# Heads' last norm in an RWKV-7 layer: logarithms and exponentials in groups of four, gates and norm products moved to later steps

## The reference, cut to what matters

```python
mean = jnp.mean(ys, axis=-1, keepdims=True)
var = jnp.mean(jnp.square(ys - mean), axis=-1, keepdims=True)
yn = ((ys - mean) * lax.rsqrt(var + GN_EPS)).reshape(B, T, D)
yn = yn * p['rwkv_lnx_g'][i].astype(F32) + p['rwkv_lnx_b'][i].astype(F32)
bonus = (jnp.sum(rh * kh * p['rwkv_rk'][i].astype(F32), axis=-1, keepdims=True) * vh).reshape(B, T, D)
out = ((yn + bonus).astype(u.dtype) * g) @ p['rwkv_wo'][i]
```

## Time and profile before

| | |
|---|---|
| device time, median of 3 runs | 3728.64 us (3728.14 to 3729.97) |
| profiled execution: its time, its span | 3730.17 us, 3728.4 us |
| mean granted TensorE clock over the span | 0.949 |
| TensorE busy over the span | 3406.7 us, 91% |
| VectorE, ScalarE busy over the span | 1154.4 us (31%), 908.2 us (24%) |
| this stage: first mean product, end of the last product | 2651.83 us, 2877.88 us |
| its steps without a projection | 2651.8 to 2725.4 us |

### The profile page before, as it was taken

One profiled execution on the slowest core, in us unless ns is written; L12 is line 12 of the kernel. 1 busy time (PEld: TensorE's weight loads), 2 busy tenths in 40 slices (PEclk: granted clock), 3 DMA queues, 4 the chain that ended last, 5 costly groups with the idle time before them and its releaser, 6 DMA issues. The chain is left out here.

```text
span 3728.4 us, 65930 instructions
## 1 busy us (share of the span) xinstructions
PE 3406.7 (91%) x29166; PEld 2836.6 (76%) x29166; DVE 1154.4 (31%) x1968; ACT 908.2 (24%) x1542; POOL 460.2 (12%) x375
## 2 busy tenths in 40 slices
PE   5999687879999999979999699998899799999996
PEld 3667354559999999946555399998455799999995
DVE  1099653131111111151445333433232311112112
ACT  2001234122111111110245333332252311111111
POOL 0000110001122122100011111110000122122120
PEclk9999898889999999989999799999589899999998
DMA  2123342111111111112032322221300111111111
GB/s 79 51 49 96 123 159 92 34 34 40 46 49 48 37 54 46 35 35 87 31 135 104 124 45 55 51 46 50 122 0 1 46 41 51 42 52 49 37 46 61
DMA packets 171994, 222.35 MB, mean 60 GB/s; under 512 B 104739, under 2 KB 122916, under 8 KB 170692
## 3 DMA queue, kind: packets, MB, share of 16 engines
q1 hardware_dynamic: 159284, 174.42, 15.8%
q0 software_dynamic: 12432, 43.80, 3.3%
HBM read 180.63 MB, written 37.55 MB: 59 GB/s over the span
## 5 line engine op out<-in xcount | busy, mean ns | idle before, releaser
L2415 PE MATMUL f_out<-f_u_hi,f_weights_hi 128*128 128x352 f32 x2112 | 685.4, 325 | 48.0 <-DVE f_u_lo L2457 48.0
L2416 PE MATMUL f_out<-f_u_lo,f_weights_hi 128*128 128x352 f32 x2112 | 680.4, 322 | 0.0
L2417 PE MATMUL f_out<-f_u_hi,f_weights_lo 128*128 128x352 f32 x2112 | 679.9, 322 | 0.0
L2391 POOL TENSOR_TENSOR f_weights_lo<-f_weights,f_weights_hi 128x1024 fp32r<-128x1024 f32 (+2 forms) x168 | 323.1, 1924 | 1731.2 <-ACT f_weights_hi L2427 1731.2
L2415 PEld LDWEIGHTS f_out<-f_u_hi,f_weights_hi 128*128 128x128 f32 x2112 | 399.2, 189 | 50.2 <-issue 40.8
L1292 PE MATMUL rf_out<-rf_mixed,rf_weights 128*128 128x352 f32 (+2 forms) x1344 | 413.7, 467 | 24.0 <-DVE rf_mixed L1451 24.0
L2416 PEld LDWEIGHTS f_out<-f_u_lo,f_weights_hi 128*128 128x128 f32 x2112 | 399.7, 189 | 0.0
L2417 PEld LDWEIGHTS f_out<-f_u_hi,f_weights_lo 128*128 128x128 f32 x2112 | 398.7, 189 | 0.0
L1292 PEld LDWEIGHTS rf_out<-rf_mixed,rf_weights 128*128 128x128 f32 (+2 forms) x1344 | 246.9, 186 | 185.7 <-issue 49.6
L2415 PE MATMUL f_out<-f_inner_hi,f_weights_hi 128*128 128x352 f32 x1056 | 341.4, 323 | 4.0 <-DVE f_inner_lo L2488 4.0
L2480 DVE TENSOR_TENSOR f_product<-f_out,f_gate 128x352 f32<-128x352 f32 x132 | 69.3, 525 | 880.3 <-PE f_out L2417 880.3
(11 more groups left out here) (348 smaller groups left out, 4467.7 us busy)
## 6 DMA issues: line engine op xcount, KB each, us to landing
f_weights<-in_w_gu SPq DMA_DIRECT2D x88, 512.0 KB, 3.5
f_weights<-in_w_down SPq DMA_DIRECT2D x48, 256.0 KB, 2.6
rf_weights<-in_w_rkv SPq DMA_DIRECT2D x24, 512.0 KB, 3.6
f_weights<-in_w_down SPq DMA_DIRECT2D x32, 320.0 KB, 2.9
all_hT<-in_x SPq DMA_DIRECT2D x2, 4224.0 KB, 13.0
all_hT<-in_cache_k SPq DMA_DIRECT2D x32, 256.0 KB, 4.7
all_hT<-in_cache_k POOLq DMA_DIRECT2D x32, 256.0 KB, 4.3
all_hT<-in_cache_v SPq DMA_DIRECT2D x32, 256.0 KB, 3.6
```

The source lines that it names most:

```text
L2391: pool.tensor_tensor(lo[:, s, :w], raw[:, s, :w], hi[:, s, :w].bitcast(F32), ALU.subtract).then_inc(lo_ready, 1)
L2415: pe.matmul(out, hi[:, s, w], x_hi, start=(k == 0), stop=False)
L2416: pe.matmul(out, hi[:, s, w], x_lo, start=False, stop=False)
L2417: last = pe.matmul(out, lo[:, s, w], x_hi, start=False, stop=(k == parts - 1))
```

## The change

The step lags become GATE = 4, NORM = 5 and LAG = 14, with GROUP = 4. TensorE's step s is then mean_sum(s), gates(s-4), project(s-14), var_sum(s-1). VectorE's is centre(s+1), add(s-15), norm(s-5). ScalarE's is square(s+1), log(s), and in every fourth step the four exponentials of the group; before it was one logarithm and one exponential in each step. The ring of centred tiles has 10 slots in place of 4, the ring of roots 8 in place of 2. Each bonus tile has its own semaphore, and unit u < 8 waits for its tile alone. The number of instructions for data stays the same on every engine, and so do the DMAs and their order.

```diff
+GROUP = 4
...
     UNITS_ = NCH * KD
-    LAG = KD + 3
+    GATE, NORM, LAG = GROUP, GROUP + 1, KD + GROUP + 2
...
-        d, sq, stat = st.sb("centred", [P, 4, TC]), st.sb("sq", [P, 2, TC]), st.sb("stat", [P, 2, TC])
+        DB, SB = 2 * GROUP + 2, 2 * GROUP
+        d, sq, stat = st.sb("centred", [P, DB, TC]), st.sb("sq", [P, 2, TC]), st.sb("stat", [P, SB, TC])
...
+        bonus_in = [st.sem(f"bonus_loaded{i}") for i in range(KD)]
...
-                    sp.dma_start(bonus[:, i], scratch["bonus"][i]).then_inc(q_["bonus_loaded"], 16)
+                    sp.dma_start(bonus[:, i], scratch["bonus"][i]).then_inc(bonus_in[i], 16)
...
                     if s < UNITS_:
                         mean_sum(s)
-                    if 0 <= s - 1 < UNITS_:
-                        gates(s - 1)
+                    if 0 <= s - GATE < UNITS_:
+                        gates(s - GATE)
                     if s >= LAG:
                         project(s - LAG)
                     if 0 <= s - 1 < UNITS_:
...
+                def log(u):
+                    act.wait_ge(q_["var_sum"], u + 1)
+                    if u >= SB:
+                        act.wait_ge(q_["n1"], u - SB + 1)
+                    act.activation(stat[:, u % SB], var[u % 2][:, :TC], ACT.Ln, scale=1.0 / DH,
+                                   bias=K.gn_eps).then_inc(q_["log"], 1)
+
                 def root(u):
-                    act.wait_ge(q_["var_sum"], u + 1)
-                    if u >= 2:
-                        act.wait_ge(q_["n1"], u - 1)
-                    act.activation(stat[:, u % 2], var[u % 2][:, :TC], ACT.Ln, scale=1.0 / DH,
-                                   bias=K.gn_eps).then_inc(q_["log"], 1)
                     act.wait_ge(q_["log"], u + 1)
-                    act.activation(stat[:, u % 2], stat[:, u % 2], ACT.Exp, scale=-0.5).then_inc(q_["root"], 1)
+                    act.activation(stat[:, u % SB], stat[:, u % SB], ACT.Exp, scale=-0.5).then_inc(q_["root"], 1)
 
                 square(0)
-                for u in range(UNITS_):
-                    if u + 1 < UNITS_:
-                        square(u + 1)
-                    root(u)
+                for s in range(UNITS_):
+                    if s + 1 < UNITS_:
+                        square(s + 1)
+                    if s < UNITS_:
+                        log(s)
+                        if s % GROUP == GROUP - 1:
+                            for u in range(s - GROUP + 1, s + 1):
+                                root(u)
...
                     if u < KD:
-                        dve.wait_ge(q_["bonus_loaded"], 16 * KD)
+                        dve.wait_ge(bonus_in[u], 16)
...
                 for s in range(UNITS_ + LAG):
                     if s + 1 < UNITS_:
                         centre(s + 1)
-                    if s >= LAG:
-                        add(s - LAG)
-                    if s < UNITS_:
-                        norm(s)
+                    if s > LAG:
+                        add(s - LAG - 1)
+                    if 0 <= s - NORM < UNITS_:
+                        norm(s - NORM)
+                add(UNITS_ - 1)
```

More of the change, by code:

```diff
@@ L2142, in finish_heads @@
         g2, g2b = st.sb("gate2", [P, KD, P]), st.sb("gate2b", [G2, KD, P])
-        d, sq, stat = st.sb("centred", [P, 4, TC]), st.sb("sq", [P, 2, TC]), st.sb("stat", [P, 2, TC])
+        DB, SB = 2 * GROUP + 2, 2 * GROUP
+        d, sq, stat = st.sb("centred", [P, DB, TC]), st.sb("sq", [P, 2, TC]), st.sb("stat", [P, SB, TC])
         mean, var, gate, out = ([st.bank(f"{n}{s}") for s in range(2)] for n in ("mean", "var", "gate", "out"))
         q_ = {n: st.sem(n) for n in ("mean_sum", "centred", "sq", "var_sum", "log", "root", "n1", "n2", "gate", "gated",
-                                     "projected", "added", "gates_loaded", "bonus_loaded", "weights_loaded")}
+                                     "projected", "added", "gates_loaded", "weights_loaded")}
+        bonus_in = [st.sem(f"bonus_loaded{i}") for i in range(KD)]
         col = lambda n, i: vec[:, VEC.at[n]][:, i:i + 1]
@@ L2213, in square @@
                         act.wait_ge(q_["var_sum"], u - 1)
-                    act.activation(sq[:, u % 2], d[:, u % 4], ACT.Square).then_inc(q_["sq"], 1)
-                def root(u):
-                    act.wait_ge(q_["var_sum"], u + 1)
-                    if u >= 2:
-                        act.wait_ge(q_["n1"], u - 1)
-                    act.activation(stat[:, u % 2], var[u % 2][:, :TC], ACT.Ln, scale=1.0 / DH,
-                                   bias=K.gn_eps).then_inc(q_["log"], 1)
+                    act.activation(sq[:, u % 2], d[:, u % DB], ACT.Square).then_inc(q_["sq"], 1)
+                def log(u):
[4 more added lines that the diff above has]
+                                   bias=K.gn_eps).then_inc(q_["log"], 1)
+                def root(u):
                     act.wait_ge(q_["log"], u + 1)
-                    act.activation(stat[:, u % 2], stat[:, u % 2], ACT.Exp, scale=-0.5).then_inc(q_["root"], 1)
+                    act.activation(stat[:, u % SB], stat[:, u % SB], ACT.Exp, scale=-0.5).then_inc(q_["root"], 1)
                 square(0)
-                for u in range(UNITS_):
-                    if u + 1 < UNITS_:
-                        square(u + 1)
-                    root(u)
+                for s in range(UNITS_):
[6 more added lines that the diff above has]
+                                root(u)
             @block.vector
@@ L2235, in centre @@
                     dve.wait_ge(q_["mean_sum"], u + 1)
-                    dve.scalar_tensor_tensor(d[:, u % 4], mean[u % 2][:, :TC], -1.0 / DH, yT[:, i, cols],
+                    dve.scalar_tensor_tensor(d[:, u % DB], mean[u % 2][:, :TC], -1.0 / DH, yT[:, i, cols],
                                              ALU.mult, ALU.add).then_inc(q_["centred"], 1)
@@ L2241, in norm @@
                     dve.wait_ge(q_["root"], u + 1)
-                    dve.scalar_tensor_tensor(d[:, u % 4], d[:, u % 4], col("lnx_g", i), stat[:, u % 2],
+                    dve.scalar_tensor_tensor(d[:, u % DB], d[:, u % DB], col("lnx_g", i), stat[:, u % SB],
                                              ALU.mult, ALU.mult).then_inc(q_["n1"], 1)
                     if u < KD:
-                        dve.wait_ge(q_["bonus_loaded"], 16 * KD)
+                        dve.wait_ge(bonus_in[u], 16)
                     dve.wait_ge(q_["n1"], u + 1)
-                    dve.scalar_tensor_tensor(d[:, u % 4], d[:, u % 4], col("lnx_b", i), bonus[:, i, cols],
+                    dve.scalar_tensor_tensor(d[:, u % DB], d[:, u % DB], col("lnx_b", i), bonus[:, i, cols],
                                              ALU.add, ALU.add).then_inc(q_["n2"], 1)
@@ L2250, in norm @@
                     dve.wait_ge(q_["n2"], u + 1)
-                    dve.tensor_tensor(yT[:, i, cols], gate[u % 2][:, :TC], d[:, u % 4], ALU.mult).then_inc(q_["gated"], 1)
+                    dve.tensor_tensor(yT[:, i, cols], gate[u % 2][:, :TC], d[:, u % DB], ALU.mult).then_inc(q_["gated"], 1)
                 def add(w):
```

## The result

The changed kernel takes 3788.38 us (median of 4 runs, 3780.24 to 3789.89), the kernel before in the same session 3728.39 us. The ratio is 1.0161, 95% interval 1.0146 to 1.0177: 60 us slower. The forecast was 3783, range 3757 to 3799. All ratios here leave out one execution of the kernel with filler products (further on), which took 4505.87 us at a mean clock of 0.735, where its nine others took 3733 to 3744.

What follows compares the result with a forecast made beforehand. From 2725.4 on TensorE's own products bound the stage; before that, waits between engines. 2731.7 + 14.7 + 94.2 + 18.0 + 6.9 + 18.9 + 47.8 = 2932.2 against 2877.9, +54.3 us, hence 3783 us, range 3757 to 3799.

Steps and rivals of the forecast that it cites:

- The loop: Steps 6 to 23: TensorE's gate product waits for a norm queued behind centring that needs this step's mean; 8.09 us at half clock.
- The start and the first stretch: Steps 0 to 5 end at 2667; steps 6 to 13 at half clock take 64.7 us, so step 14 begins at 2731.7.
- The steps with a projection: Steps 15 to 23: 94.2 us at full clock plus 18.0 for clock falls, 2.0 a step; step 14 apart, 14.7.
- every fall is paid in full: Rival: each clock fall in steps 15 to 23 costs 3.99 us, not 2.0; 3807 us, chance 0.10.
- the one that I called likeliest: Half clock in the first steps and a clock fall in most waits; 3783 us, own range 3771 to 3799, chance 0.60.
- The rest: End of the stage: step 24 at 6.89 us, steps 25 to 27 at 6.30 each, last ten projections 47.78.
- ScalarE at nothing: Grouping removes 36 of 48 table loads; ScalarE needs 2.2 us a unit, less than any TensorE step, so costed at nothing.
- Full clock in the projections: Rival: same loop, but no clock falls between projections; 3765 us, chance 0.19.
- Full clock in both stretches: Rival: TensorE at full clock before and during the projections; +9 us, 3738 us, chance 0.05.
- The faster case (3714): Rival: TensorE runs through without waiting for the gate, steps of 5.66 us; -15 us, 3714 us, chance 0.06.
- The 46 us for table loads on the path: ScalarE: if each of the 36 removed loads had been on the path, 46.2 us off, 3682; not in the sum.
- The estimate of 96 us: ScalarE: with a drain of about 1.38 us a load, removing 36 would bring about 96 us, 3633; not in the sum.

Runs made afterwards that it cites:

- filler products: Changed kernel with six more unread 160-column products behind the mean product in steps 6 to 22; 3738.34 us, 1.0036 to the kernel before.
- GATE 5: Changed kernel with GATE 5 in place of 4, nothing else; 3683.38 us, 0.9890 to the kernel before.
- norm first: Changed kernel with VectorE's norm(s-5) ahead of centre(s+1), GATE still 4; 3684.72 us, 0.9893 to the kernel before.
- the ungrouped run: Changed kernel with each exponential right after its logarithm, 48 table loads in place of 12; 3793.15 us, 1.0184 to the kernel before.
- the run with GATE 5 and no grouping: Changed kernel with GATE 5 in place of 4 and each exponential right after its logarithm; 3700.41 us, 0.9935 to the kernel before.
- the groups of one: Changed kernel with GROUP 1, GATE 2, NORM 2, LAG 11 and two more slots for centred tiles; 3692.08 us, 0.9909 to the kernel before.
- the bonus part: Kernel before with only a semaphore for each bonus tile, waited for tile by tile; 3724.51 us, 0.9999 to the kernel before.

## Why the prediction was right

**The loop.** Right in place and size. 18 waits were forecast at 2.3 to 3.0 us, some 45 in all; there are 18, of 2.35 to 2.79, 46.4 in all. The step at half clock was worked out as 8.09 and is 8.08. That it is the cause is shown from both ends: GATE 5 and norm first each remove it, and each gives 3683 to 3685.

**The start and the first stretch.** mean_sum(6) was put at 2667 and came at 2664.23, since the clock rose early; the first step of the loop still ran mostly at full clock. So step 14 began at 2726.29 and not at 2731.7: 5.4 us too much. Step 14 itself was put at 14.7 and took 14.54 (2726.29 to 2740.83).

**The steps with a projection.** This is the term that was mis-sized. Steps 15 to 23 were put at 94.2 us at full clock plus 18.0 for falls of the clock, 112.2. They took 123.6 us (mean product of step 15 at 2740.83, gate product of step 24 at 2864.40). The 94.2 is borne out by the filler run, 10.54 for 10.52. So the falls cost 29.4 us, 3.3 a step and not 2.0: I had supposed that some waits would pass without one. None did, not even in step 15, whose wait is no longer than the 2.36 that had been followed by full clock in the earlier trace rows:

```profile
2743.94 0.86 PE L2188 MATMUL hw_gate<-c_lora,hw_gate 128*128 128x352 f32 x2 [2.36 <-DVE c_yT L2263]
...
2744.73 1.54 PE L2189 MATMUL hw_gate<-c_lora_g,hw_gate2b 32*128 32x352 f32 x2
```

In a step such as the one shown in the result, the gates take 0.94 more and the projection 2.47, 3.4 of the 3.99 that had been the upper bound. The case that every fall is paid in full (3807) was nearer to this term than the one that I called likeliest.

**The rest.** 73.6 us from there to the end of the last projection were forecast, 73.3 measured. The two errors, 5.4 us too much and 11.4 too little, cancel in part: 2932.2 forecast, 2937.72 measured. That it came so near is luck. With only one of the two terms right the forecast would have been 3778 or 3794, both still in the range.

**ScalarE at nothing.** Right for the step times, and nearly so for the whole: 5 to 7 us by the ungrouped run. Putting nothing on the 36 loads that went was right only because the loop hid them; with the loop open they are worth 17 us at lag 14.

**The rivals.** Full clock in the projections (3765) didn't occur in any of the nine steps. Full clock in both stretches (3738) is nearly what the filler products brought about: 3738.34, with a stage of 239.1 us against 235.2 in that case. The faster case (3714) needed the gate not to wait. Its mechanism is what GATE 5 makes real, and there its price was too small: the clock didn't stay at half, so 3683 and not 3714. The 46 us for table loads on the path are far above the 17 that 36 loads brought, since beside projections ScalarE has time to spare. The estimate of 96 us, worked out with the drain of about 1.38 us a load that the Trainium skill gives in "ScalarE: Activation LUTs", What ACT_TABLE_LOAD costs, is further off. The ungrouped runs don't agree with such a drain: a unit takes 4.06 us on ScalarE with 2 x 1.283 for loads and three operations of some 0.5, and in the lines of its queue above the logarithm starts 1.29 us after the start of its load and the next load 0.57 after that, which leaves no room for 1.38 more.

## What to carry to other kernels

When a step is moved in several in-order queues, write down for each wait which instruction of which step releases it and what stands ahead of that one in its own queue: if anything there needs the current step of the waiting engine, the two engines take turns, and one more step of lag at one end opens it. Price a wait of TensorE with its clock: here the waits by themselves cost some 52 us beside the same kernel with the loop open, and the half clock that they brought on as much again. And look at the order of the queues before the work in them: some 33 of the 41 us to be had came from later norms and gates, with no table load taken away.

## What was not expected of the hardware

In the nine steps 15 to 23 of the changed kernel (13.4 to 13.8 us, one wait each, of 2.36 us in the first and 2.79 in the others) the granted clock fell every time and came back in every projection; the stretches of 6.7 us shown above are 1.00 and 0.50 by turns. Filled with short products up to a remaining wait of 0.73 to 1.16, it stayed up but for one projection, and fell again behind the one wait of 2.79 that had no fillers. Waits of 1.24 in steps of 4.06 were followed by half clock once too (2687.5 to 2693.5 in the run with GATE 5 and no grouping), and in the groups of one so were waits of 0.87, 0.87, 0.47 and 0.50 within 9 us (0.54 from 2672.5 to 2676.2). So the length of one wait doesn't tell whether the clock falls: 2.36 was followed by 1.00 in the earlier trace rows and by 0.50 here.

Nor does the idle time in a step. With 0.92 us idle in most steps of 6.58 the kernel before stayed at half from 2673.8 to 2725.3; with 0.80 idle in steps of 5.46 the filler kernel stayed at full from 2664 to 2707. What makes the difference was not tested.

The same stage begins at times between 2643.16 and 2651.94 us in the ten profiled executions, although nothing ahead of it differs. Those 9 us lie in earlier parts of the kernel and are larger than the effect of the bonus part. Compare the stage's own length before reading a few us into the total.
